# Sums of weight blocks made in DRAM by accumulating DMAs during the first stage of a hybrid decoder step, with the down product run combination by combination

## What is computed

```python
    z = rmsnorm(x) @ w_in            # 1024 x 3120, the first stage of the kernel
    ...
    x = x + mix @ lp['w_out']
    hid = jax.nn.relu(rmsnorm(x, lp['norm2_g']) @ lp['w_up'])     # 1024 x 4096
    x = x + (hid * hid) @ lp['w_down']                            # 4096 x 1024
```

## Time and profile before

| | us |
|---|---|
| median of 3 runs (1909.62 to 1911.67) | 1909.99 |
| the profiled execution, own time | 1903.13 |
| its span, first to last instruction | 1901.4 |
| mean granted clock of TensorE | 0.958 of full |
| TensorE busy (matmuls), 13909 recorded | 1705.2 (90%) |
| VectorE / ScalarE / GpSimd busy | 1266.3 / 810.1 / 690.5 |
| moved by DMA | 300.55 MB, mean 158 GB/s |

### The profile page before, as it was taken

How to read it: one execution, slowest core, us unless ns; L and a number is a source line. 1 busy time by engine, 2 the same in 40 slices (tenths; PEclk the granted TensorE clock), 3 DMA queues, 4 the chain that set the end, 5 groups by cost and what they waited for, 6 DMA issues and landing times. The chain is left out here.

```text
span 1901.4 us, 35561 instructions
## 1 busy us (share of the span) xinstructions
PE 1705.2 (90%) x13909; PEld 1558.3 (82%) x13909; DVE 1266.3 (67%) x1958; ACT 810.1 (43%) x1565; POOL 690.5 (36%) x568
## 2 busy tenths in 40 slices
PE   7799999989999989999769868888888879999998
PEld 6799999968888768887449868888887879888998
DVE  6363584268777666667775887777777847666665
ACT  6333332156655454443533434444344424333334
POOL 1000000022222252231124544455444458777776
PEclk9899999989999989999889979899999989999999
DMA  7841265250000177766956224555555895555522
GB/s 173 116 101 34 57 166 167 90 156 23 14 1 2 45 247 241 236 221 180 205 191 201 91 64 177 210 190 192 187 190 190 302 390 214 220 216 216 217 95 94
DMA packets 223492, 300.55 MB, mean 158 GB/s; under 512 B 58238, under 2 KB 166390, under 8 KB 220702
## 3 DMA queue, kind: packets, MB, share of 16 engines
q1 hardware_dynamic: 218638, 260.20, 43.3%
q0 software_dynamic: 2304, 33.56, 4.6%
q10 hardware_dynamic: 2384, 4.53, 1.0%
HBM read 198.81 MB, written 103.63 MB: 159 GB/s over the span
## 5 line engine op out<-in xcount | busy, mean ns | idle before, releaser
L59 PE MATMUL pm<-ops,slots 128*128 128x258 f32 x1792 | 527.3, 294 | 109.9 <-DVE onat L3783 52.5
L60 PE MATMUL pm<-ops,slots 128*128 128x258 f32 x1792 | 519.6, 290 | 0.0
L61 PE MATMUL pm<-ops,slots 128*128 128x258 f32 x1792 | 517.1, 289 | 0.0
L59 PEld LDWEIGHTS pm<-ops,slots 128*128 128x128 f32 x1792 | 350.5, 196 | 124.4 <-DVE slots L3764 57.0
L61 PEld LDWEIGHTS pm<-ops,slots 128*128 128x128 f32 x1792 | 353.2, 197 | 0.0
L60 PEld LDWEIGHTS pm<-ops,slots 128*128 128x128 f32 x1792 | 352.8, 197 | 0.0
L59 PE MATMUL pz<-hH,winH 128*128 128x344 f32 x600 | 200.2, 334 | 1.7 <-DVE hL L850 1.7
L60 PE MATMUL pz<-hL,winH 128*128 128x344 f32 x600 | 193.9, 323 | 0.0
L61 PE MATMUL pz<-hH,winL 128*128 128x344 f32 x600 | 193.9, 323 | 0.0
L3764 DVE TENSOR_TENSOR slots<-uact,slots 128x512 fp32r<-128x512 f32 x128 | 116.0, 906 | 103.4 <-ACT slots L3555 103.4
L3917 DVE TENSOR_TENSOR onat<-pm,onat 128x516 f32<-128x516 f32 x144 | 99.8, 693 | 83.2 <-ACT wo L3592 44.6
(11 more groups left out here) (658 smaller groups left out, 3936.1 us busy)
## 6 DMA issues: line engine op xcount, KB each, us to landing
hidD_scratch<-onat SPq DMA_DIRECT2D x112, 516.0 KB, 2.9
ops<-hidD_scratch SPq DMA_DIRECT2D x56, 1032.0 KB, 10.4
uact<-in_w_up_dram SPq DMA_DIRECT2D x16, 1024.0 KB
uact<-in_w_down_dram SPq DMA_DIRECT2D x16, 1024.0 KB
raw<-in_w_in_dram SPq DMA_DIRECT2D x24, 512.0 KB, 3.7
hold<-vS_scratch SPq DMA_DIRECT2D x4, 2048.0 KB, 11.1
zT_scratch<-zb ACTq DMA_DIRECT2D x8, 516.0 KB, 2.6
hold<-in_x_prompt_dram SPq DMA_DIRECT2D x8, 512.0 KB, 3.8
```

Of the source, the lines that this page charges most:

```text
L59: nc.tensor.matmul(out, wH, mH, start=start and k == 0, stop=False)
L60: nc.tensor.matmul(out, wH, mL, start=False, stop=False)
L61: last = nc.tensor.matmul(out, wL, mH, start=False, stop=stop and k == n - 1)
```

## The change

**First stage.** After its copy at L192, GpSimd issues 32 DMAs of 2 MB each on its own queue. For `w_up` and then for `w_down`: eight plain copies of blocks from DRAM to DRAM make the start of the four sums (`begin`), eight accumulating DMAs add a second block to them in DRAM (`add`, two of the sums get another sum added). `slot(s)` holds each until the s-th block of `w_in` has landed; `add` also waits for what the sum consists of. All of them are additions; the signs are moved into the formulas of `evict` and `take`. SyncE waits for the sums before the mixer's weight loads.

**Mixer.** GpSimd's `add_weights`, `add_hidden` and `accumulate` are gone. Weights come one operand at a time, 256 KB, into three buffers `raw[n % 3]`, a plain block from `w_up` or `w_down` and a sum from DRAM. The up product's results rotate through all four PSUM tensors. The four sums of hidden blocks are made on VectorE (`first_sum`, `middle_sums`, `last_sum`), and hidden operands are stored unsplit (258 KB) and split after they are loaded (`high_hid`, `low_hid` on pieces of 2 x 128 features). The down product has j outermost, then m, then four steps t over the 4096 features' sixteen block rows, added up in PSUM: 28 results of 96 matmuls are taken out in place of 224 of 12, all by VectorE. Output tiles are turned and stored as they become final, from combination 2 on. The number of matmuls with 258 columns is the same.

```diff
+SUM_ROW = 2048
...
                 pool.wait_ge(z_copied, whole(2))
                 nc.gpsimd.tensor_copy(umtail[:, :, :], um[:, :, T:T + 3]).then_inc(um_kept, 1)
+                for which in range(2):
...
+                    def begin(f, block):
+                        for rows in half:
+                            nc.gpsimd.dma_start(sums[f, rows, :], block[rows, :], max_dma_last_dim=SUM_ROW).then_inc(done[f], 16)
+                    def add(f, n, block):
+                        pool.wait_ge(done[f], 32)
+                        nc.gpsimd.dma_start(sums[f, half[n], :], block[half[n], :], accum_op=ALU.add, max_dma_last_dim=SUM_ROW).then_inc(done[f], 16)
+                    def slot(s):
+                        pool.wait_ge(raw_in, RAW0 + 16 * (12 * which + s))
+                    slot(1)
+                    begin(0, block_of(1, 0))
...
+                    pool.wait_ge(done[2], 64)
+                    for n in range(2):
+                        slot(11 + n)
+                        add(3, n, sums[2, :, :])
...
-                def add_weights(v):
...
-                def add_hidden(p):
...
-                def accumulate(M):
...
+                def load_weights(n):
+                    if n >= 3:
+                        sp.wait_ge(wL_ready, n - 2)
+                    sp.dma_start(raw[n % 3].rearrange("p (k n) -> p k n", k=4), weights_at(n)).then_inc(w_in[n % 3], 16)
...
-                    for j in range(7):
-                        if M % 2 == 0:
-                            pe.wait_ge(wL_ready, 7 * v + j + 1)
-                        if m == 0:
-                            pe.wait_ge(hid_in[g % 2][j], 16 * (g // 2 + 1))
...
+                for u in range(16 * 7):
+                    j, m, t = u // 16, u // 4 % 4, u % 4
+                    pe.wait_ge(wL_ready, NUP + u + 1)
+                    if m == 0:
+                        pe.wait_ge(hidL_ready, 2 * (4 * j + t) + 2)
+                    if t == 0:
+                        free_room(pe, down_product(j, m))
+                    down(j, m, t)
...
+                def middle_sums(p):
+                    dve.wait_ge(bA_ready, 2 * p + 2)
+                    if p:
+                        dve.wait_ge(hid_stored[3], 16 * p)
+                        dve.wait_ge(hid_stored[1], 16 * p)
+                    nc.vector.drain()
+                    nc.vector.tensor_tensor(T3, C22, C12, ALU.subtract).then_inc(t_ready, 1)
+                    nc.vector.tensor_tensor(T2, C22, T1, ALU.subtract).then_inc(t_ready, 1)
...
+                for p in range(1, NPAIR + 1):
+                    for j in range(7 if p < NPAIR else 3):
+                        if j == 0:
+                            evict(p - 1, 6, None if p > 1 else 1)
+                            relu2(C12)
+                            first_sum(p - 1)
+                        elif j == 1:
+                            middle_sums(p - 1)
+                        elif p < NPAIR:
+                            evict(p, j - 1)
+                        if j == 6:
+                            relu2(C21)
+                        low_w(7 * p + j + 4)
```

More of the change, by code:

```diff
@@ new lines, in room, with free_room, weights_at @@
+        def room(s):
+            return whole[place(s)]
+        def free_room(eng, s):
+            before = [n for n in range(max(s - 6, 0), s) if place(n) == place(s)]
+            if before:
+                last = before[-1]
+                if last < 7 * (NPAIR + 1) and last % 7 == 0:
+                    eng.wait_ge(evA, last // 7 + 1)
+                else:
+                    eng.wait_ge(evD, evicted(last))
+        def weights_at(n):
+            if n < NUP:
+                f, cols = n % 7, slice(n // 7 * P, n // 7 * P + P)
+                if f in SUM_OF:
+                    return up_sums[SUM_OF[f], :, :, cols]
+                second = slice(NPAIR * P + cols.start, NPAIR * P + cols.stop)
+                return w_up[int(f != 0), :, :, second if f == 5 else cols]
+            f, m, at = (n - NUP) // 16, (n - NUP) // 4 % 4, slice(n % 4 * 4, n % 4 * 4 + 4)
+            cols = slice(m * P, m * P + P)
+            if f in SUM_OF:
+                return down_sums[SUM_OF[f], :, at, cols]
+            second = slice(NM * P + cols.start, NM * P + cols.stop)
+            return w_down[int(f != 0), :, at, second if f == 5 else cols]
@@ L3692, in _ @@
+                for u in range(16 * 7):
+                    high_w(NUP + u + 4)
+                    high_pieces(NUP + u)
+                    done = u - 6
+                    if done >= 0 and done % 4 == 0 and done // 16 in FINAL:
+                        copy_out(4 * FINAL.index(done // 16) + done // 4 % 4)
+                copy_out(15)
             @block.vector
@@ L3742, in inverse @@
                     dve.wait_ge(rt_done, c + 1)
[L3743 to L3744 removed]
+                    if h is None:
+                        nc.vector.reciprocal(whole[3], both(rn))
+                    else:
+                        nc.vector.reciprocal(whole[3][:, h, :], part(rn, h))
                 def scale_x(c, k):
@@ L3994, in program @@
             keep["late_z"] = nc.alloc_semaphore("late_z_stored")
+            keep["weight_sums"] = [[nc.alloc_semaphore(f"sums_{which}{n}") for n in range(4)] for which in ("up", "down")]
             project_and_prepare(nc, io, keep)
```

791 lines of the change are left out of this document (331 added, 460 removed).

## The result

The changed kernel takes **1922.5 us** (median of 9 runs, 1917.9 to 1935.6) against 1909.6 us (9 runs, 1904.2 to 1912.3) in the same comparison: ratio **1.008**, 95% interval 1.006 to 1.010. It is slower by 0.8%, clear of the noise of the runs, where 1789 us and a range of 1760 to 1858 had been forecast. Its profiled execution took 1918.35 us, with a span of 1916.6, 15.2 us more than before.

A forecast was written before the change was run, and what follows sets the result against it. The mixer's products were taken as bound by TensorE's gaps and lowered clock, from one raw-weight buffer and late VectorE. Terms -127 - 4 + 10 = -121 gave 1782 us profiled, 1789 us as a median; range 1760 to 1858.

The forecast's parts named there:

- first stage, +10: First stage up to its barrier: the 32 background DMAs nearly fit its 300 us of room; +10 us, ends 0 and +62.
- Mixer's products, -127: Channel mixer's up and down products: TensorE becomes the bound, 640 us in place of 767, -127 us.
- pair 0, -4: 1087 to 1127 us: GpSimd's sums of weights beside VectorE's splits of x go; 0 to -9 us, taken as -4.
- Rival B: Mixer gets another bound, from small loads behind stores and pieces or VectorE's waits for stores; 1834 us, chance 10%.
- Tail, 0: After the last matmul: still an addition, turns, a copy and a store; 0, within 1 us either way.
- 960 to 1087 us, 0: Stretch before pair 0: the same matmuls, with six weight loads queued for later; 0 us.
- Price of an addition, 1 to 2 copies: First stage's accumulating DMAs in DRAM: 16 take 90 us as copies, up to 180 with a second read.
- Issue on GpSimd, 1.04 to 7.4 us each: First stage: issuing the DMAs costs GpSimd 33 to 237 us of the 300, covered by its idle time.
- the first stage's end beyond 395 us: Sign of a wrong forecast: first stage ends this late with GpSimd last, pointing to dear additions in DRAM.
- Told apart by an addition's landing, 11 or over 17 us: Sign for 2 MB additions: 11 us means double price, over 17 us means additions much slower than reads explain.
- Landings of w_in above 20 us: Sign of a wrong forecast: w_in loads land this late, with TensorE waiting for them before 384 us.
- A: Rival: additions in DRAM take double, so the first stage's barrier is +30 to +62 us late; 1829 us, chance 25%.

## Why the prediction was wrong

The step that failed is the term **first stage, +10** (measured +130), in its last sentences: "Loads of w_in land in 3.7 us and have a whole block (12 to 14 us) to spare; at three times that they would still be hidden." There is one raw buffer, `raw`. The next load is issued when VectorE has made the low part, so the load's slack is a block less the two splits (1.06 us on ScalarE and 1.23 on VectorE in the mean, with handing over about 2.5). With blocks of 12.2 to 15.3 us that is 10 to 13 us, where three times 3.7 is 11 and the measured landing 14.4; 14.4 and 2.5 make the block of 17 us that was measured. The sum had only engine time in it, and never asked what one load meets when it arrives beside an addition. Its 64 packets per engine (512 KB / 512 bytes / 16) pass one for one with those of the addition, as the counts above show. My estimate from this, 64 x (0.19 + 0.03) = 14.1 us, comes close in part by luck: the load's first packets come some 4 us after its issue, then about 50 pairs pass at 0.194 us until the addition is through (10 us), and the rest follow in 0.4. Why the first packets come 3 us later than alone stays open. The Trainium skill, "DMA: Bandwidth & Descriptors", section "Queues, rings and completion order", says that each engine goes round the queues that have work, a whole packet at a time. The trace agrees in the turns, with 494 packets of one queue for 495 of the other and 14.4 us for a load beside additions; how many packets pass in one turn no run here shows. This rule should have stood beside the term.

Point by point:

- *Mixer's products, -127, and pair 0, -4*: measured -124.5 together, right to 7 us. Busy 98 to 99% at 0.99, VectorE's 128x516 instructions at 0.68 to 0.70 us; a sum of such blocks (no row before) took 0.696 where I took 0.69. The steps behind it, by line and form, 1257 to 1560 us of the changed kernel:

```profile
L3700 DVE TENSOR_TENSOR slots<-uact,slots 128x512 fp32r<-128x512 f32 x104 | 71.2, 684 | 0.9 <-ACT slots L3521 0.9
...
L3758 DVE TENSOR_TENSOR onat<-onat 128x516 f32<-128x516 f32 x15 | 10.4, 696 | 1.4
...
L3723 DVE TENSOR_TENSOR onat<-onat,pm 128x516 f32<-128x516 f32 x14 | 9.7, 692 | 11.0 <-PE pm L61 11.0
```

  VectorE now waits for TensorE, not the other way round. Rival B is out.
- *Tail, 0*: -1.1. *960 to 1087 us, 0*: some +5; the run without sums has 603.3 us from the barrier to the first matmuls of `mix_and_mixer` where before it is 599.2, so 4 of the 5.9 come without the sums' DMAs; their cause was not looked for.
- *Price of an addition, 1 to 2 copies*: 2.06. It was the upper end. The Trainium skill, "Collectives: The Full Stack", section "The bandwidth ceiling: the fold count and why AG ≠ RS ≠ AR", puts the add of ReduceScatter at half a copy's rate for its second read; the trace agrees in the size, 190 ns for 2 KB against 183 ns for 4 KB. The copy's own term, 90 us for 16, measured 96. The barrier by my own sum for the double price would have been 46 us late. That sum also let the last two additions lie behind the barrier (22 us), and the run with rows of 512 bytes has GpSimd leave the stage only when the last has landed: without that term it is 68. With the measured engine times and no overlap of packets it is 404 - 303 = 101. So the price explains somewhere between 46 and 101 of the 130 us, an estimate; no run makes the additions cheap without changing the landings beside them. That the landings cost time by themselves is shown where the engine time did fit: half of the sums, 69 us late, and copies only, 79.
- *Issue on GpSimd, 1.04 to 7.4 us each*: 0.76 to 1.0 for a copy, 1.3 to 1.8 for an addition; no loss was traced to it.
- *The signs*: "the first stage's end beyond 395 us" came true. "Told apart by an addition's landing, 11 or over 17 us" would have misled: additions landed in 16.4 us in the median while their engine time was 12.4. "Landings of w_in above 20 us" came true for two loads (49.9 and 22.0) but was set too high for the others, since 14.4 are enough.
- *The chances*: slower had 9%, all of it on additions at three times a copy or more. The case that came (double price, plus a load with a single buffer in the same stage) was not among the rivals: A had the price without the load.

## What to carry to other kernels

A background transfer is not free because the engines have idle time: for each load that runs beside it, set its landing *beside one such transfer* against its slack, which with one buffer is the length of a step less the time to empty the buffer. Place bulk transfers in a stage whose loads are few or far ahead, at most one at a time and better one that is through before the next load is issued, and never several at once beside a load that is waited for. Count the packets that stand ahead of that load in its own queue too: small ones take turns with the bulk transfer like large ones. And where a change consists of a gain and of a preparation elsewhere in the program, run each half alone: -115 and +127 were both large, and their sum nearly hid them.

## What was unexpected in the hardware

- A load of 512 KB in 512-byte packets from one queue lands in 3.7 us alone, in 14.4 us beside a single 2 MB addition from another, and in 50 to 65 us when eight 2 MB copies are queued there at once. The packets of the two queues pass one for one, whatever their size: 494 of 512 bytes for 495 of 2 KB, 786 of 512 bytes for 789 of 512, 1456 of under 512 bytes for 1456 of 4 KB. So 18 of the 50 us are small loads that stand ahead in the same queue, and some 20 stay open. The issue of such a small load on SyncE also took up to 7.9 us in place of 0.6, and that of the load itself 9.3 in place of 0.4.
- One copy of 2 MB beside a load is not free either: in the run with the additions moved, the four loads issued 2 to 3 us behind a copy, from 281 to 325 us, landed in 10.2 to 15.0 us. The median of all 16 loads from 94 to 330 us is 6.4 only because seven were issued when the copy was through or nearly so (3.5 to 4.3 us). Such landings fit the slack almost everywhere, and the stage ended 2.7 us later than before.
- An accumulating DMA within DRAM costs 190 ns for 2 KB per engine, 2.06 times a copy of the same bytes, and cutting it into rows of 512 bytes raises GpSimd's time to issue it from 1.3-1.8 us to 2.9-4.8 us.
